# Sparse attention of a hybrid transformer: where the softmax is normalised, and which engine copies the turned weights

## The reference, cut to what matters

```python
def dsa_attention(h, w_in, idx_k_norm, w_o, cos, sin, n_keys):
    ...
        top_val, top_idx = lax.top_k(score, topk)
        valid = top_val > -jnp.inf
        ks = gather(k, top_idx)
        vs = gather(v, top_idx)
        s = jnp.einsum('bqhd,bqjhd->bhqj', qb, ks).astype(f32)
        s = jnp.where(valid[:, None], s, -jnp.inf)
        p = jax.nn.softmax(s, axis=-1)
        return jnp.einsum('bhqj,bqjhd->bqhd', p.astype(vs.dtype), vs)
    o = sweep_blocks(block, T)
    return o.reshape(B, T, DSA_QKV) @ w_o
```

## Time and profile before

| what | value |
|---|---|
| runs, us | 1808.78, 1803.48, 1805.46 (median 1805.46) |
| the profiled execution | 1798.56 us, span 1796.8 us, mean granted clock 0.975 |
| TensorE, VectorE, ScalarE, GpSimd busy in the span | 1713.8, 949.0, 632.5, 330.8 us |
| chain that ended last | TensorE 76%, VectorE 7% |
| sparse attention | from 1279.56 to 1358.87 us |

### The profile page before, as it was taken

How to read it: one execution, slowest core, us unless ns; L and a number is a source line. 1 busy time by engine, 2 the same in 40 slices (tenths; PEclk the granted TensorE clock), 3 DMA queues, 4 the chain that set the end, 5 groups by cost and what they waited for, 6 DMA issues and landing times.

```text
span 1796.8 us, 33090 instructions
## 1 busy us (share of the span) xinstructions
PE 1713.8 (95%) x14293; PEld 1537.7 (86%) x14293; DVE 949.0 (53%) x1881; ACT 632.5 (35%) x1095; POOL 330.8 (18%) x450
## 2 busy tenths in 40 slices
PE   7999989979998899999999999999899999999997
PEld 3777679859996589999999998799669999999886
DVE  5237695435335865655562115787883555565003
ACT  3354442243114653222222222322584322222222
POOL 0001102001220012222222222122012222222221
PEclk9999969899998999999999999999999999999999
DMA  7521400126994039898888999699305888898995
GB/s 301 177 76 59 176 1 4 61 53 145 226 207 93 1 69 195 181 180 184 180 184 185 199 194 203 145 212 210 79 2 111 175 184 186 181 185 182 197 209 139
DMA packets 81794, 266.46 MB, mean 148 GB/s; under 512 B 11648, under 2 KB 15360, under 8 KB 81520
## 3 DMA queue, kind: packets, MB, share of 16 engines
q0 software_dynamic: 59040, 214.98, 56.7%
q1 hardware_dynamic: 18592, 43.57, 7.0%
q10 hardware_dynamic: 4016, 5.78, 1.1%
HBM read 252.49 MB, written 2.10 MB: 142 GB/s over the span
## 4 chain that ended last, share of the span: by engine, by line
PE 76%; DVE 7%; issue 2%; DMA 1%; ACT 1%; POOL 0%; ACTq 0%; DVEq 0%; POOLq 0%
PE banks L603 21%; PE banks L604 20%; PE banks L605 20%; PE banks L2090 3%; PE banks L656 1%; PE banks L669 1%; DMA w_lo<-in_weights 1%; DVE stat L1407 1%; PE banks L689 1%; PE banks L1845 1%; PE banks L1847 1%; PE banks L1846 1%; PE banks L732 1%; PE banks L945 1%; DVE arena L1417 1%
## 5 line engine op out<-in xcount | busy, mean ns | idle before, releaser
L603 PE MATMUL banks<-hn_hi,w_hi 128*128 128x264 f32 (+2 forms) x2216 | 637.9, 288 | 14.4 <-DMA w_lo<-in_weights 12.8
L604 PE MATMUL banks<-hn_lo,w_hi 128*128 128x264 f32 (+2 forms) x2216 | 631.4, 285 | 0.0
L605 PE MATMUL banks<-hn_hi,w_lo 128*128 128x264 f32 (+2 forms) x2216 | 630.8, 285 | 0.0
L1049 ACT ACTIVATE w_lo<-w_hi 128x1024 fp32r<-128x1024 f32 x205 | 217.2, 1060 | 771.9 <-DMA w_hi<-in_weights 757.3
L603 PEld LDWEIGHTS banks<-hn_hi,w_hi 128*128 128x128 f32 x2216 | 419.0, 189 | 26.8 <-issue 22.3
L604 PEld LDWEIGHTS banks<-hn_lo,w_hi 128*128 128x128 f32 x2216 | 420.2, 190 | 0.7 <-issue 0.2
L605 PEld LDWEIGHTS banks<-hn_hi,w_lo 128*128 128x128 f32 x2216 | 417.9, 189 | 0.3
L1004 POOL DMA_DIRECT2D w_hi<-in_weights x205 | 114.1, 557 | 915.3 <-PE banks L605 840.3
L1011 POOL DMA_DIRECT2D w_lo<-in_weights x205 | 180.8, 882 | 156.1 <-ACT w_lo L1049 146.8
L603 PE MATMUL banks<-a_hi,w_hi 128*128 128x264 f32 (+1 forms) x506 | 160.4, 317 | 1.6 <-DVE u_in L1576 0.8
L604 PE MATMUL banks<-a_lo,w_hi 128*128 128x264 f32 (+1 forms) x506 | 160.8, 318 | 0.0
(11 more groups left out here) (426 smaller groups left out, 2702.5 us busy)
## 6 DMA issues: line engine op xcount, KB each, us to landing
w_hi<-in_weights POOLq DMA_DIRECT2D x205, 512.0 KB, 5.2
w_lo<-in_weights POOLq DMA_DIRECT2D x205, 512.0 KB, 7.2
ring<-in_weights SPq DMA_DIRECT2D x49, 512.0 KB, 4.5
arena<-arena ACTq DMA_DIRECT2D x64, 66.0 KB, 5.3
arena<-arena SPq DMA_DIRECT2D x64, 66.0 KB, 4.9
arena<-in_gate_w SPq DMA_DIRECT2D x8, 512.0 KB, 3.5
h<-in_xT SPq DMA_DIRECT2D x2, 1024.0 KB, 6.3
arena<-in_alibi SPq DMA_DIRECT2D x1, 1024.0 KB, 7.7
```

Of the source, the lines that this page charges most:

```text
L603: mm(o, w[0][:, j, :], x[0][:, k, lo:hi], start=first, stop=False)
L604: mm(o, w[0][:, j, :], x[1][:, k, lo:hi], start=False, stop=False)
L605: ins_ = mm(o, w[1][:, j, :], x[0][:, k, lo:hi], start=False, stop=last)
L1049: nc.scalar.activation(split_at(n)[1], split_at(n)[0].bitcast(F32), ACT.Copy, scale=-1.0).then_inc(S["w_negated"], 1)
```

## The change

The weights are turned without being normalised. `transposes(v)` waits for the exponentials (`a_exp`) and no longer for `a_prob`. `normalise` becomes `inverse`, which makes the reciprocals alone. `values(v)` ends with two more matmuls that spread the two heads' reciprocals over 64 partitions each, into columns 128 to 255 of the output's bank; it waits for `a_inv` as well. `out(v)` copies 256 columns to a ring of four buffers, and GpSimd multiplies the two halves into `oT`. The `None` units are scaled by VectorE when they are copied from PSUM. Turned copies of n = 1 and 3 go to VectorE, after `soft(v+3)`; n = 0, 2 and `None` stay on ScalarE. GpSimd's rests stand between its multiplies, at the places of `RESTS_AFTER`, and `high` waits for the multiplies. Two semaphores are saved by counting in others: `meta_in` in `cond_in`, `g_zero` in `zeroed`.

```diff
+    def inverses(v, c):
+        return stat[:, v % 4, 4 + c:5 + c].to_broadcast([P, 64])
+    def raw_out(v):
+        return sq_flat[:, v % 4 * 2 * P:(v % 4 + 1) * 2 * P]
+    RESTS_AFTER = {21: 0, 22: 1, 23: 2, 24: 3, 25: 4, 29: 5, 32: 6, 33: 7}
+    def is_wide(v):
+        p, n = DSA_UNITS[v]
+        return p is not None and n in (1, 3)
...
             def transposes(v):
-                pe.wait_ge(S["a_prob"], DA_N + v + 1)
-                pe.wait_ge(S["a_pt"], DA_N + v)
+                pe.wait_ge(S["a_exp"], 2 * DA_N + v + 1)
+                if v:
+                    pe.wait_ge(*dsa_copied(v - 1))
...
             def values(v):
-                pe.wait_ge(S["a_pt"], DA_N + v + 1)
+                pe.wait_ge(*dsa_copied(v))
                 if v >= 2:
                     pe.wait_ge(S["a_o"], outputs_done(v - 2))
+                pe.wait_ge(S["a_inv"], v + 1)
...
+                    for c in range(2):
+                        last = mm(psum[64 * c:64 * c + 64, 6 + v % 2, P:2 * P], inverses(v, c), ident[:, :], start=True, stop=True)
                 last.then_inc(S["a_pv"], 1)
...
-        def output_rests(base):
+        def dsa_outputs():
+            def scale(v):
+                p, n = DSA_UNITS[v]
+                pool.wait_ge(S["a_o"], outputs_done(v))
+                x = raw_out(v)
+                g.tensor_tensor(oT[:, p, n * P:(n + 1) * P], x[:, 0:P], x[:, P:2 * P], ALU.mult).then_inc(S["o_scaled"], 1)
+            def rest(k):
+                pool.wait_ge(S["o_hi"], KT + k + 1)
                 g.tensor_tensor(o_lo[:, k, :], oT[:, k, :], o_hi[:, k, :].bitcast(F32), ALU.subtract).then_inc(S["o_split"], 1)
+            for v in range(len(DSA_UNITS)):
+                if v not in LAST_AT:
+                    scale(v)
+                if v in RESTS_AFTER:
+                    rest(RESTS_AFTER[v])
...
             def copy(v):                                  # ScalarE
+                if is_wide(v):
+                    return
...
             def high(first, end):                         # ScalarE
-                    act.wait_ge(S["a_o"], outputs_done(max(DSA_UNITS.index((p, 3)), LAST_AT[1])))
+                    act.wait_ge(S["a_o"], outputs_done(LAST_AT[1]))
+                    act.wait_ge(S["o_scaled"], scaled_done(DSA_UNITS.index((p, 3))))
...
-            def normalise(v):
+            def inverse(v):
                 ve.wait_ge(S["a_exp"], 2 * DA_N + v + 1)
-                st.link(V.reciprocal(stat[:, v % 4, 4:4 + heads], stat[:, v % 4, 2:2 + heads]))
-                for c in range(heads):
-                    x = dsa_prob(v, c)[:, 0:T2 if p is None else keys(n)]
-                    last = V.tensor_scalar(x, x, stat[:, v % 4, 4 + c:5 + c], None, ALU.mult)
-                last.then_inc(S["a_prob"], 1)
+                V.reciprocal(stat[:, v % 4, 4:4 + heads], stat[:, v % 4, 2:2 + heads]).then_inc(S["a_inv"], 1)
+            def copy(v):                                  # VectorE, wide units
+                ve.wait_ge(S["a_tr"], DA_N + v + 1)
+                if v >= 2:
+                    ve.wait_ge(S["a_pv"], values_done(v - 2) - (v - 2 in LAST_AT))
+                V.tensor_copy(pt2[:, v % 2, :, 0:w], psum[:, 4:6, 0:w]).then_inc(S["a_pt_wide"], 1)
...
             def out(v):
-                    V.tensor_copy(oT[:, p, n * P:(n + 1) * P], src).then_inc(S["a_o"], 1)
+                    if v >= 4:
+                        ve.wait_ge(S["o_scaled"], scaled_done(v - 4))
+                    V.tensor_copy(raw_out(v), psum[:, 6 + v % 2, 0:2 * P]).then_inc(S["a_o"], 1)
...
-        sp.dma_start(h[:, :, 0:META], ins["metaT"]).then_inc(S["meta_in"], 16)
+        sp.dma_start(h[:, :, 0:META], ins["metaT"]).then_inc(S["cond_in"], 16)
...
-        act.wait_ge(S["cond_in"], 16)
+        act.wait_ge(S["cond_in"], 32)
         A(cond, cond, ACT.Silu).then_inc(S["c_silu"], 1)
```

More of the change, by code:

```diff
@@ L290, in build @@
     sq = sb("sq", [P, 2, T2])
+    sq_flat = sq.rearrange("p a t -> p (a t)")
     hn_hi_flat, hn_lo_flat = (x.rearrange("p k t -> p (k t)") for x in (hn_hi, hn_lo))
@@ L376, in build @@
                 r_done x1_done
-            rope_in rope_read rope_done v_ch v_tr v_tok a_sc a_max a_exp a_prob a_tr a_pt a_pv a_o
+            rope_in rope_read rope_done v_ch v_tr v_tok a_sc a_max a_exp a_inv a_prob a_tr a_pt a_pt_wide a_pv a_o o_scaled
             hd_sq hd_sum hd_var hd_std hd_tr o_last_tr o_last_hi o_last hd_done res_done u_evac conv_done silu_done a_ready
@@ L547, in values_done, with scaled_done, dsa_copied @@
         return DA_N + v + 1 + sum(x <= v for x in LAST_AT)
+    def inverses(v, c):
+        return stat[:, v % 4, 4 + c:5 + c].to_broadcast([P, 64])
+    def raw_out(v):
+        return sq_flat[:, v % 4 * 2 * P:(v % 4 + 1) * 2 * P]
+    def scaled_done(v):
+        return v + 1 - sum(x <= v for x in LAST_AT)
+    RESTS_AFTER = {21: 0, 22: 1, 23: 2, 24: 3, 25: 4, 29: 5, 32: 6, 33: 7}
+    def is_wide(v):
+        p, n = DSA_UNITS[v]
+        return p is not None and n in (1, 3)
+    def dsa_copied(v):
+        wide = sum(is_wide(x) for x in range(v + 1))
+        return (S["a_pt_wide"], wide) if is_wide(v) else (S["a_pt"], DA_N + v + 1 - wide)
     def outputs_done(v):
@@ L660, in transposes @@
                 p, n = DSA_UNITS[v]
-                pe.wait_ge(S["a_prob"], DA_N + v + 1)
-                pe.wait_ge(S["a_pt"], DA_N + v)
+                pe.wait_ge(S["a_exp"], 2 * DA_N + v + 1)
+                if v:
+                    pe.wait_ge(*dsa_copied(v - 1))
+                else:
+                    pe.wait_ge(S["a_pt"], DA_N)
                 if p is None:
@@ L970, in dsa_o_free @@
             pe.wait_ge(S["a_max"], DA_N + 2 * len(DSA_UNITS))
-            pe.wait_ge(S["a_pt"], DA_N + len(DSA_UNITS))
+            pe.wait_ge(*dsa_copied(len(DSA_UNITS) - 1))
         residual(S_DSAO, 16, dsa_o_free, KEPT)
@@ L1030, in pool_block2 @@
             if n == S_DSAO:
-                output_rests(8)
+                dsa_outputs()
             high_load(n + W_RING)
@@ L1228, in ffn @@
             product_high(FT - 1)
-        act.wait_ge(S["meta_in"], 16)
+        act.wait_ge(S["cond_in"], 32)
         for k in range(KT):
@@ L1395, in da_attention @@
                 ve.wait_ge(scattered[b], 128 * 4)
-            ve.wait_ge(S["zeroed"], 2)
+            ve.wait_ge(S["zeroed"], 3)
             for par in range(2):
@@ L1508, in normalise @@
                 ve.wait_ge(S["a_exp"], 2 * DA_N + v + 1)
-                st.link(V.reciprocal(stat[:, v % 4, 4:4 + heads], stat[:, v % 4, 2:2 + heads]))
-                for c in range(heads):
-                    x = dsa_prob(v, c)[:, 0:T2 if p is None else keys(n)]
-                    last = V.tensor_scalar(x, x, stat[:, v % 4, 4 + c:5 + c], None, ALU.mult)
-                last.then_inc(S["a_prob"], 1)
+                V.reciprocal(stat[:, v % 4, 4:4 + heads], stat[:, v % 4, 2:2 + heads]).then_inc(S["a_inv"], 1)
+            def copy(v):
+                if not is_wide(v):
+                    return
+                w = keys(DSA_UNITS[v][1])
+                ve.wait_ge(S["a_tr"], DA_N + v + 1)
+                if v >= 2:
+                    ve.wait_ge(S["a_pv"], values_done(v - 2) - (v - 2 in LAST_AT))
+                V.tensor_copy(pt2[:, v % 2, :, 0:w], psum[:, 4:6, 0:w]).then_inc(S["a_pt_wide"], 1)
             def out(v):
@@ L1519, in out @@
                     ve.wait_ge(S["a_pv"], values_done(v) - 1)
-                    V.tensor_copy(last_rows_sb[:, v % 2, :], src).then_inc(S["a_o"], 1)
+                    ve.wait_ge(S["a_inv"], v + 1)
+                    V.tensor_scalar(last_rows_sb[:, v % 2, :], src, stat[:, v % 4, 4:5], None, ALU.mult).then_inc(S["a_o"], 1)
                 else:
                     ve.wait_ge(S["a_pv"], values_done(v))
-                    V.tensor_copy(oT[:, p, n * P:(n + 1) * P], src).then_inc(S["a_o"], 1)
+                    if v >= 4:
+                        ve.wait_ge(S["o_scaled"], scaled_done(v - 4))
+                    V.tensor_copy(raw_out(v), psum[:, 6 + v % 2, 0:2 * P]).then_inc(S["a_o"], 1)
             def out_last(v):
@@ L1539, in dsa_attention @@
                 if v < N:
-                    normalise(v)
+                    inverse(v)
                 if v + 3 < N:
                     soft(v + 3)
+                if v < N:
+                    copy(v)
                 if v - 3 in LAST_AT:
@@ L1693, in vector_block2 @@
                 if i == 16:
-                    ve.wait_ge(S["zeroed"], 3)
+                    ve.wait_ge(S["zeroed"], 4)
                     for c in range(2):
@@ L2260, in _ @@
         pool.wait_ge(S["slot_used"], S_IN1 + N_IN1)
-        g.memset(g_at, 0.0).then_inc(S["g_zero"], 1)
+        g.memset(g_at, 0.0).then_inc(S["zeroed"], 1)
         pool.wait_ge(S["s1_out"], 16)
@@ L2653, in g_take @@
             if lv == 0:
-                ve.wait_ge(S["g_zero"], 1)
+                ve.wait_ge(S["zeroed"], 2)
             for hd in range(0, 4, 2):
```

6 lines of the change are left out of this document (2 added, 4 removed).

## The result

The changed kernel takes 1806.33 us (median of 15 runs) against 1801.42 for the kernel before (15 runs, interleaved with it). The ratio is 1.0030, 95% interval 1.0017 to 1.0043: +5.4 us (3.1 to 7.7) where +4.2 was forecast; the two medians themselves lie 4.9 apart. The profiled execution is 1805.32 us with a span of 1803.5.

What follows compares the result with a forecast made beforehand. TensorE was taken to bound the sparse attention's full passes. Spreads at +6.98 us less 1.1, 1.0 and 0.7 of gains gave +4.2, 1802.8 us profiled and 1809.6 carried over to the median; range 1802 to 1815.

Steps and rivals of the forecast that it cites:

- The sum: Whole kernel: +6.98 for the spreads, -1.1, -1.0 and -0.7 of gains, together +4.2 us.
- TensorE bounds the full passes: Sparse attention, full passes of four units: TensorE busy for all 8.53 us, so relieving VectorE there gains nothing by itself.
- the spread costs its columns: End of each values group on TensorE: two more matmuls cost 0.218 us per unit, 32 units, +6.98 us.
- Rival A: Full passes: VectorE was the real pacemaker, so relief pays more than the spread costs; -2.8 us, 1802.7; chance 0.17.
- The third wait at the values: Values groups on TensorE: also waiting for the reciprocals costs 0, though up to 1.6 us was possible.
- The renamed semaphores: Silu of cond, which now waits for the meta tokens as well: these are issued long before, so 0.
- The head: Start of the stage: unit 1's transposes no longer wait for the normalising multiply, -1.1 us.
- The middle: Transposes of units 22 and 23: their waits for VectorE's stretched multiplies, 0.99 us together, go; -1.0 us.
- The drain: Last units of the stage, with no scores left: TensorE's waits shrink from 1.60 to 0.87 us, -0.7.
- Rival B: End of each values group: the spread costs more than its columns, 0.29 to 0.37 per unit; 1812.1 to 1814.5; chance 0.20.
- Rival C: VectorE's in-order queue: turned copies come late, 0.5 us in each of eight passes; +8.1 in all, 1813.6; chance 0.10.
- GpSimd and the tail: GpSimd's 32 multiplies at 0.54 us; work after the last values lasts 3.2 to 3.8 us, hidden before the projection.

Runs made afterwards that it cites:

- e3: The changed kernel with every spread of the reciprocals issued twice; 1811.09 us in one run, stage 91.29 us.
- e1: The changed kernel with the reciprocals spread for the first two units only, other outputs scaled with stale columns; 1802.74 us, ratio 1.0003 to the kernel before.
- e2: The changed kernel with VectorE making the output copies before the turned copy in each round; 1805.04 us, ratio 1.0018 to the kernel before.
- e8: e2 with reciprocals widened to 128 columns by GpSimd and spread by one transpose instead of two matmuls; 1802.51 us, ratio 1.0011 to the kernel before.
- e6: The kernel before with its normalising multiplies moved to GpSimd and the output's low parts to VectorE, no spread; 1811.61 us, ratio 1.0054.
- e7: e2 with all copies of turned weights on ScalarE again; 1805.93 us, ratio 1.0015 to the kernel before.

## Why the prediction was right

**The sum** was +4.2, the ratio says +5.4 (3.1 to 7.7): right in sign and near in size. That nearness is in part luck. Of the 2.8 us of gains in the sum only 0.9 came (0.54, 0.0 and 0.33, below), and the stage grew by 6.1; the one large term, which was right, hides it, and an interval of 4.6 us can't tell 4.2 from 6.1. The time forecast, 1809.6, was carried over from three runs with a median of 1805.46; fifteen have 1801.42, so the level was some 4 us high and the difference is what can be judged. The low end of the interval, 0.17%, also tells the slowdown from no change, which the prediction had thought out of reach below 0.3%.

**TensorE bounds the full passes; the spread costs its columns.** 6.98 us, the main term. Right: 0.22 in every unit and 9.40 for the pass; e3 gives 0.44 for two; e1 without it is back at the time before. Rival A needed a VectorE that paces the passes. Its busy time fell from 7.38 to 6.63 and no piece but the spread changed. 7.1 had been expected, from a sum of single lengths; but busy counts instructions that overlap once (the groups of this pass add up to 8.7), and so "adds its instructions", said of it ahead of the prediction, is not exact.

**The third wait at the values**: 0, right, since the pieces V are as they were. **The renamed semaphores**: 0, not tried by itself. The stage begins at 1279.42 to 1283.69 in the three traces with the old names and at 1280.10 to 1284.76 in the seven with the new ones; in such a scatter an effect of a microsecond wouldn't show.

**The head, -1.1: mis-sized, -0.54 in the profiled execution** (9.22 against 9.32 to T(3), with 0.44 of spreads in it). The wait went as the step says. What I priced without looking is the level at which TensorE's freed work runs: the low level lasted two microseconds longer, through T(1), whose piece was 0.92 where e2's is 0.59. e1, with an early rise, has -1.37.

**The middle, -1.0: the waits named are gone, a new one of 0.97 took their place.** The step stepped through transposes, scores, values and the copies, and left out the turn of unit 17, an instruction of its own that waits for an output. e2 removes it by order alone.

**The drain, -0.7: -0.33.** Two of the three waits came out (0.33 for 0.31, 0.23 for 0.21); V(33) was priced from its copy, 0.35, and had 0.71, since it also waits for `out(31)`. e2 has 0.37.

**Rival B** is out by e3: 0.22 per unit and no fixed part.

**Rival C** was the right mechanism with the wrong place: a copy that waits, ahead of an output that could run. I had given it half a microsecond in each full pass (and its 1813.6 lies inside the range up to 1815, not just short of it); there slack hides it, and it bit in two places, at a turn and at values that come once. The two cost 1.3 of the 1.9 us between +6.1 and +4.2; the head's clock is nearly all of the rest.

**GpSimd and the tail**: 0.46 per multiply for 0.54; after the last values 0.43, 0.46, 0.65 and 1.33 with small gaps end 3.46 behind the stage (3.2 to 3.8 forecast), hidden.

**What stays open**: why the clock rises 3.0 us after the stage's start in one profiled execution and 9.4 in another. The two late ones, e8 (9.4) and e6 (9.5), are those in which GpSimd works at the head; the other eight rose at 3.0 to 5.4. But e6's TensorE also waits there, and in after and e7, whose heads are nearly e2's, the clock rose 0.7 us later than in e2. It was not tried, as one execution of each can't separate the kernel from chance. No version here that computes the right output beats the kernel before, and e8, the nearest, can't be told from it; to win it would need its remaining 32 x 0.11 = 3.5 us of spread to be outweighed by gains that the forecast put at 2.8.

## What to carry to other kernels

Work moved from a hidden engine to the one that bounds is paid in full wherever that engine isn't waiting anyway, however small each piece is: 0.22 us 32 times was 7.0 us, and what it relieved was idle time at three edges of the stage, which gave 0.9 back. When a copy joins an in-order queue, list every waiter of what stands behind it, above all those that come only once (a last unit's turn, the drain), and put what can already run ahead of what must wait. A long broadcast was cheap as a copy (290 ns, on GpSimd) and dear as a reciprocal (942 ns, on VectorE), so widen after computing.

## What the runs showed of the hardware

- A reciprocal on VectorE takes 155 ns for 2 columns and 942 ns for 128; GpSimd's broadcast copy of the same 128 columns takes 290 ns.
- GpSimd multiplies two tensors of 128 columns in 458 ns, but one tensor by a column of scalars in 617 (1564 for 512), where VectorE's multiply by a scalar had a median of 415 over all sizes.
- Between two groups on TensorE whose weights have different shapes lies a gap of 0.12 us or more in the weight loads, mostly 0.17, and none where the shape stays. So transposes behind a turned spread cost 0.15 us less than behind values (0.22 against 0.37 for two, 0.87 against 1.02 for eight).
- In the same place of nearly the same program the granted clock rose from 0.50 to 1.00 between 3.0 (e1) and 9.4 us (e8) after the stage's start; in e8 that moved the stage by 1.8 us, a third of the effect under study. A single profile of a stage behind idle time has to be cut where the clock has settled.
